# Running an expert's third matrix unit by unit beside the next expert's first two, with eight slots in the weight ring

## The chip, the cores and the metric

One core of a Trainium2 chip runs the whole kernel. The metric is device time in microseconds, the median of a few executions. Durations below come from one profiled execution.

## The reference

A two-layer block, then two layers of a second kind, for 256 tokens of width 1024 in fp32. The change touches only the mixture of experts in the second layer of the first block:

```python
def swiglu(x, w1, w3, w2):
    return (jax.nn.silu(x @ w1) * (x @ w3)) @ w2

def moe_ffn(x, router_w, w1, w3, w2):      # x: 256 x 1024, 8 experts, top 2
    logits = (xt @ router_w).astype(F32)
    top_v, top_i = lax.top_k(logits, TOP_K)
    top_w = jax.nn.softmax(top_v, axis=-1)
    gates = jnp.sum(jax.nn.one_hot(top_i, N_EXPERTS, dtype=F32) * top_w[..., None], axis=1)
    for e in range(N_EXPERTS):             # w1, w3: 1024 x 3584, w2: 3584 x 1024
        y = y + gates[:, e:e + 1] * swiglu(xt, w1[e], w3[e], w2[e])
```

## The kernel before

**Precision.** A weight block is used as a high and a low part. ScalarE copies the raw fp32 block into the high part (fp32r), VectorE subtracts it from the raw block and writes the low part over the raw one. Tokens are split likewise. A product then takes three matmuls: token high x weight high, token high x weight low, token low x weight high (`products`, L920).

**Units.** Expert weights come in units of 1 MB (128 x 2048 fp32), issued by SyncE in the order of use. An expert has 42: 28 for its first two matrices (w1, w3) and 14 for the third (w2). The raw ring has nine slots (`EXPERTS`, a `Ring`): seven of its own, the buffer `bias2` and the buffer `gain`. `gain` is away in rounds 2 and the start of 3, since round 2 keeps its hidden rows there, and again from unit 273 of 336 on (`GAIN_LENT`). The high parts have four slots, and both ScalarE (`ahead`, L1904) and VectorE (`split`, L2516) go at most three units ahead of TensorE (`EXPERT_LEAD`). A slot is free when TensorE has used its unit.

**Rounds.** Experts are sorted by how many tokens chose them. Even rounds r = 0, 2, 4, 6 take the larger ones, with up to 128 gathered tokens: 4 weight blocks a unit, 3 matmuls of 512 columns each, 12 in all. Odd rounds (`few`) take the smaller ones, with up to 64 tokens. There the token high parts fill 64 rows of the array's output and the low parts the other 64 (`gathered_few`), so 2 matmuls a block, 8 a unit, give all products. Round 2 (`LARGE`) does both for the largest expert: 20 a unit. Further rounds stand behind a branch and don't run with these inputs.

**A round, on TensorE.** `pair_e` (or `pair_few`, and for round 2 `many_tokens_e`) goes through w1 and w3 in tiles of 512 hidden columns, two tiles at a time in PSUM banks `tile0` to `tile3`. A finished tile goes through ScalarE (silu) and VectorE (product), and two units later TensorE transposes it (`turn`, L1045) into one of four `aux` banks, from where ScalarE and VectorE write it as hidden parts. In odd rounds ScalarE copies both raw tiles out and TensorE folds the two halves while it transposes (`fold_hidden`, L1389). When all seven tiles are through, the 14 units of w2 run, with their sums in `tile2` and `tile3`. ScalarE scales the output with the gate (`back_out`), VectorE adds the low part in odd rounds (`back_low`).

**Between rounds.** The output of round r - 1 is scattered back to token order behind unit 2 of round r (`scatter`, L1368, four banks), VectorE adds it to `acc` (L3068). The gates are turned behind unit 4 (`turn_gates`, L1351 and L1354), and in the rounds that gather, unit 4 of w2 is followed by the gather of the next one or two rounds' tokens (`gather`, L1340, eight banks in one go). Round 1 gathers for rounds 2 and 3, round 3 for 4 and 5, round 5 for 6 and 7.

Each engine has its own instruction stream and runs it in order; the order is written out by hand, and the streams meet in semaphores (`unit_done`, `high_ready`, `low_ready`, `aux_full`, `aux_evac`, `ye_ready`). The main loop of an odd round on TensorE shows the manner:

```python
for pair in range(PAIRS):
    def meanwhile(k):
        if k == TURN_AFTER and pair == 0:
            scatter_last(r)
        if k == TURN_AFTER and pair > 0:
            fold_hidden(2 * pair - 2)
            fold_hidden(2 * pair - 1)
        if k == PAIR_UNITS - 1 and pair == 0:
            turn_gates(r)
    pair_few(tiles[0:2], both, meanwhile)
    pair_few(tiles[2:4], both)
```

## Time and profile before

| | us |
|---|---|
| median of three executions | 2352.26 (2351.29 to 2354.27) |
| the profiled execution | 2352.72 |
| its span, first to last instruction | 2350.9 |
| the eight expert rounds | 442.0 to 1439.3 of the span |

The core's mean granted TensorE clock is 0.993. The page gives busy times over the whole span; the expert rounds are 42% of it, and the rest of the kernel is not touched. Round boundaries are the times at which TensorE's matmuls change from one expert's tokens to the next's. A matmul's own length in the timeline contains its pipeline; what it costs the stream is the distance of the starts. A row with a count merges instructions that follow each other.

### The profile page before, as it was taken

The page shows a single profiled execution, that of the slowest core. Times are in us where ns is not written, and L with a number is a line of the kernel's source. Part 1 is how long each engine was busy: PE and PEld are TensorE (multiplying, and loading weights), DVE is VectorE, ACT ScalarE, POOL GpSimd, SP SyncE. Part 2 cuts the span into 40 slices and gives each one's busy share as a digit, 9 for nine tenths or more (in the row PEclk, how much of TensorE's full clock was granted, in tenths as well). Part 3 has the DMA queues.
Part 4 walks back from the last instruction along what each step waited for, and adds up shares of the span by engine and source line. Part 5 has one row for each costly group of instructions (what it writes and reads, how often), then busy time and mean ns, then how long its engine had stood idle before and what let it go on. Part 6 is the DMA issues. An engine that isn't in the chain of part 4 may idle for free.

```text
span 2350.9 us, 29295 instructions
## 1 busy us (share of the span) xinstructions
PE 2304.0 (98%) x11179; PEld 1895.3 (81%) x11179; DVE 1810.5 (77%) x2343; ACT 1386.7 (59%) x1588; POOL 31.7 (1%) x44
## 2 busy tenths in 40 slices
PE   9999998999999999999999998999999999999998
PEld 7788887887878887788778776888888888888887
DVE  4965568798975558998999898899865669987655
ACT  4444544577865548877887785565544545654543
POOL 0000000000000000000000000000000000000000
PEclk9999999899999999999999999999999999999999
DMA  8366554699986569999999995654566565455653
GB/s 275 114 214 185 184 163 160 249 360 356 411 290 211 200 229 360 415 399 373 395 414 386 378 408 223 199 154 145 175 199 188 180 212 159 123 174 171 199 186 124
DMA packets 198508, 584.20 MB, mean 248 GB/s; under 512 B 17259, under 2 KB 26615, under 8 KB 183640
## 3 DMA queue, kind: packets, MB, share of 16 engines
q1 hardware_dynamic: 196060, 573.97, 68.8%
q0 software_dynamic: 1872, 6.82, 0.9%
q8 instruction: 91, 1.49, 0.3%
q10 hardware_dynamic: 428, 1.45, 0.2%
q14 instruction: 57, 0.47, 0.1%
HBM read 580.07 MB, written 2.12 MB: 248 GB/s over the span
## 4 chain that ended last, share of the span: by engine, by line
PE 81%; DVE 11%; ACT 6%; issue 2%; DMA 0%; POOL 0%; ACTq 0%; POOLq 0%; DVEq 0%
PE tile L922 21%; PE tile L924 21%; PE tile L923 21%; DVE units_parts L2527 5%; PE aux L1045 4%; PE aux L1389 3%; ACT high L1914 2%; PE tile L1503 2%; PE tile L1504 2%; ACT gbuf_parts L1914 1%; ACT acts L1914 1%; PE tile L1401 1%; PE aux L1786 1%; PE aux L1368 1%; DVE nat_parts L2527 1%
## 5 line engine op out<-in xcount | busy, mean ns | idle before, releaser
L2527 DVE TENSOR_TENSOR units_parts<-units,high 128x1024 fp32r<-128x1024 f32 (+3 forms) x339 | 482.6, 1442 | 94.9 <-ACT high L1914 92.0
L923 PE MATMUL tile<-units_parts,acts 128*128 128x512 f32 (+2 forms) x1352 | 518.5, 383 | 0.0
L1914 ACT ACTIVATE high<-units 128x1024 fp32r<-128x1024 f32 (+3 forms) x339 | 412.5, 1238 | 162.3 <-PE tile L924 57.0
L922 PE MATMUL tile<-high,acts 128*128 128x512 f32 (+2 forms) x1012 | 401.4, 397 | 6.3 <-DVE units_parts L2527 3.6
L924 PE MATMUL tile<-high,acts 128*128 128x512 f32 (+2 forms) x1012 | 390.3, 386 | 0.0
L923 PEld LDWEIGHTS tile<-units_parts,acts 128*128 128x128 f32 x1352 | 255.5, 189 | 46.7 <-issue 1.0
L922 PEld LDWEIGHTS tile<-high,acts 128*128 128x128 f32 x1012 | 191.2, 189 | 44.7 <-DVE units_parts L2527 6.2
L924 PEld LDWEIGHTS tile<-high,acts 128*128 128x128 f32 x1012 | 191.1, 189 | 38.8
L923 PE MATMUL tile<-units_parts,zbuf_parts 128*128 128x512 f32 x432 | 168.1, 389 | 0.0
L924 PE MATMUL tile<-high,zbuf_parts 128*128 128x512 f32 x368 | 143.3, 389 | 0.0
L922 PE MATMUL tile<-high,zbuf_parts 128*128 128x512 f32 x296 | 116.1, 392 | 0.0
L2527 DVE TENSOR_TENSOR units_parts<-units,acts 128x2048 fp32r<-128x2048 f32 x39 | 89.2, 2287 | 14.4 <-ACT acts L1914 14.3
L3279 DVE SCALAR_TENSOR_TENSOR zbuf<-cbuf,taps,zbuf 128x256 f32<-128x256 f32 x240 | 99.7, 479 | 0.0
L1945 ACT ACTIVATE acts<-aux 128x512 fp32r<-128x512 f32 x48 | 27.5, 597 | 120.8 <-PE aux L1045 120.7
L2527 DVE TENSOR_TENSOR units_parts<-units,gbuf_parts 128x2048 fp32r<-128x2048 f32 x39 | 89.2, 2287 | 11.6 <-ACT gbuf_parts L1914 11.6
L923 PEld LDWEIGHTS tile<-units_parts,zbuf_parts 128*128 128x128 f32 x432 | 81.2, 188 | 16.4
L1914 ACT ACTIVATE gbuf_parts<-units 128x2048 fp32r<-128x2048 f32 x39 | 74.7, 1916 | 29.6 <-PE tile L1403 13.0
L1914 ACT ACTIVATE acts<-units 128x2048 fp32r<-128x2048 f32 x39 | 74.8, 1918 | 12.6 <-PE tile L924 12.4
L1401 PE MATMUL tile<-high,params_parts 128*128 128x512 f32 x192 | 77.5, 404 | 3.9 <-DVE units_parts L2527 2.3
L924 PEld LDWEIGHTS tile<-high,zbuf_parts 128*128 128x128 f32 x368 | 69.1, 188 | 14.4
L2527 DVE TENSOR_TENSOR q_buf_parts<-q_buf,high 128x2048 fp32r<-128x2048 f32 x26 | 59.5, 2289 | 20.8 <-ACT high L1914 20.7
L1938 ACT ACTIVATE gbuf<-tile,row_scale 128x512 f32<-128x512 f32 x36 | 24.3, 687 | 80.7 <-PE tile L924 80.7
(565 smaller groups left out, 5078.1 us busy)
## 6 DMA issues: line engine op xcount, KB each, us to landing
units<-in_moe_w SPq DMA_DIRECT2D x156, 1024.0 KB, 8.0
units<-in_w_in SPq DMA_DIRECT2D x134, 512.0 KB, 3.9
units<-in_w_ff SPq DMA_DIRECT2D x128, 512.0 KB, 3.7
q_buf<-in_moe_w SPq DMA_DIRECT2D x39, 1024.0 KB, 7.8
k_buf<-in_moe_w SPq DMA_DIRECT2D x39, 1024.0 KB, 8.2
nat<-in_moe_w SPq DMA_DIRECT2D x39, 1024.0 KB, 8.1
bias<-in_moe_w SPq DMA_DIRECT2D x38, 1024.0 KB, 8.0
gain<-in_moe_w SPq DMA_DIRECT2D x25, 1024.0 KB, 8.4
```

The costliest lines, as they stand in the source:

```text
L922: nc.tensor.matmul(bank, lhs[0], high, start=start, stop=False)
L923: nc.tensor.matmul(bank, lhs[0], low, start=False, stop=False)
L924: return nc.tensor.matmul(bank, lhs[1], high, start=False, stop=stop)
L1045: mm = nc.tensor.transpose(bank[0:m, i * k:(i + 1) * k], src, ident[0:k, 0:k])
L1389: mm = nc.tensor.matmul(bank[:, at:at + FEW], raw[:, m, c * P:(c + 1) * P], fold[:, :], start=True, stop=True)
L1401: nc.tensor.matmul(bank[:, :], both[:, at_k, :], high[:, c, at], start=at_k == 0, stop=False)
L1503: nc.tensor.matmul(bank[:, :], both, high, start=at_k == 0, stop=False)
L1504: return nc.tensor.matmul(bank[:, :], both, low, start=False, stop=at_k == chunks - 1)
L1914: nc.scalar.activation(high_slot(SG[0], n) if wide_ else high_slot(SG[0], n)[:, 0:cols], halves(weights) if wide_ else weights[:, 0:cols], ...
L1945: nc.scalar.activation(dst, aux[k % 4][0:p, 0:n * m].rearrange("p (n m) -> p n m", n=n), ACT.Copy).then_inc(SG[0].turned_high, 1)
L2527: V.tensor_tensor(low, weights, high, ALU.subtract).then_inc(SG[0].low_ready, 1)
L3279: ins = V.scalar_tensor_tensor(y_t[:, c, :], u_t[:, c, j:j + SEQ], taps[:, c, j:j + 1], y_t[:, c, :], ALU.mult, ALU.add)
```

## The change

The rounds become steps (`step_units`). Step s runs the 28 units of the first two matrices of round s; behind each second one comes one of the 14 units of the third matrix of round s - 1. Step 0 has only first matrices, step 8 only the third matrix of round 7. The order of the loads, splits and matmuls is the same list for all engines.

The third matrix accumulates in `aux0` and `aux1`, and for the 64 further rows of round 2 in `tile2` and `tile3`; the first matrices of round 3 therefore use `tile0` and `tile1` alone. The other two `aux` banks (`spare`) serve in turn for all turns, folds, gates, scatters and gathers, with semaphores of their own (`spare_full`, `spare_evac`). A tile's turn comes behind units 9, 17 and 25 (two tiles each; in round 2 behind each fourth from 5 on), the last tile's behind unit 1 of the next step. The output of round r is scattered in step r + 2, behind units 3 and 5. A gather takes one bank behind each of the units 18 to 24 and 26 of the first matrices, for round 7's further rounds behind units 4 to 11 of its third matrix. Step 0 now has the gather for round 1, and VectorE's `find_order` behind its unit 11.

Buffers: `bias2` is no ring slot any more; it holds a third set of gathered tokens, the odd rounds' products, a selection table and scratch. The ring has eight slots with `gain`, seven without. `gain` is away in steps 2 and 3 and up to about unit 10 to 17 of step 4, and again from unit 273 on. The rules for leads (three units) and for the four high slots are the same.

```diff
--- before.py
+++ after.py
-EXPERT_COLS, EXPERT_UNITS, EXPERT_HIGHS = 2048, 9, 4
+EXPERT_COLS, EXPERT_UNITS, EXPERT_HIGHS = 2048, 8, 4
...
-GAIN_LENT = [(0, LARGE * MOE_UNITS, 1),
-             ((LARGE + 1) * MOE_UNITS + TURN_AFTER + 2 + EXPERT_OWN, (N_EXP - 2) * MOE_UNITS + MOE_UNITS // 2,
-              (LARGE + 1) * MOE_UNITS + TURN_AFTER + 2)]
-EXPERTS = Ring(ROUNDS * MOE_UNITS, (EXPERT_OWN + 1) * [[(0, ROUNDS * MOE_UNITS, 0)]] + [GAIN_LENT])
-GAIN_FREE = 1 + EXPERTS.last[EXPERT_OWN + 1]
+PAIRED, FIRST_UNITS = 2 * PAIRS * PAIR_UNITS, 2 * MOE_TILES * TILE_UNITS
+assert FIRST_UNITS == 2 * BACK_UNITS
+LAST_TILE = MOE_TILES - 1
+TAIL_AT, SCATTER_AT, GATES_AT = 1, (3, 5), 6
+CHOOSE_AT, GATHER_AT = 13, (18, 19, 20, 21, 22, 23, 24, 26)
+BACK_SCATTER, BACK_CHOOSE, BACK_GATHER = (2, 3), 2, (4, 5, 6, 7, 8, 9, 10, 11)
+STEP_UNITS = [FIRST_UNITS] + (N_EXP - 1) * [MOE_UNITS] + [BACK_UNITS]
+STEP_FIRST = [sum(STEP_UNITS[:i]) for i in range(N_EXP + 2)]
+GAIN_OPEN = STEP_FIRST[LARGE + 2] + SCATTER_AT[1] + SCATTER_AT[1] // 2 + 3
+GAIN_LENT = [(0, STEP_FIRST[LARGE], 1),
+             (GAIN_OPEN + EXPERT_OWN, (N_EXP - 2) * MOE_UNITS + MOE_UNITS // 2, GAIN_OPEN)]
+EXPERTS = Ring(ROUNDS * MOE_UNITS, EXPERT_OWN * [[(0, ROUNDS * MOE_UNITS, 0)]] + [GAIN_LENT])
+GAIN_FREE = 1 + EXPERTS.last[EXPERT_OWN]
...
+def step_units(s):
+    if s > N_EXP:
+        return [(s - 1, m) for m in range(MOE_UNITS)]
+    units = []
+    for i in range(FIRST_UNITS):
+        if s < N_EXP:
+            units.append((s, i))
+        if s > 0 and i % 2:
+            units.append((s - 1, FIRST_UNITS + i // 2))
+    return units
...
+def first_place(r, i):
+    if r == LARGE:
+        m, k = divmod(i % (2 * TILE_UNITS), TILE_UNITS)
+        return [i // (2 * TILE_UNITS)], m, k, [m]
+    if i < PAIRED:
+        pair, at = divmod(i, 2 * PAIR_UNITS)
+        m, k = divmod(at, PAIR_UNITS)
+        banks = [0, 1] if r == LARGE + 1 else [2 * m, 2 * m + 1]
+        return [2 * pair, 2 * pair + 1], m, k, banks
+    m, k = divmod(i - PAIRED, TILE_UNITS)
+    return [LAST_TILE], m, k, [m if r == LARGE + 1 else 2 * m]
+def closes(r, i):
+    return first_place(r, i)[2] == (PAIR_UNITS if r != LARGE and i < PAIRED else TILE_UNITS) - 1
...
+def turned_after(r, i):
+    if r == LARGE:
+        return [i // 4 - 1] if i >= 5 and i % 4 == 1 else []
+    return [i // 4 - 2, i // 4 - 1] if i >= 9 and i % 8 == 1 else []
...
-        gathered_few = [params_parts[:, i * 1024:(i + 1) * 1024].rearrange("p (c n) -> p c n", n=P)
-                        for i in range(2)]
+        bias2_flat, bias2_flat_parts = (v[:, :, :].rearrange("p h t -> p (h t)") for v in (bias2, bias2_parts))
+        gathered_few = [v.rearrange("p (c n) -> p c n", n=P) for v in
+                        (params_parts[:, 0:1024], params_parts[:, 1024:2048], bias2_flat_parts[:, 0:1024])]
...
+        spare = aux[2:4]
...
+            def expert(s, named):
+                for r, m in step_units(s)[EXPERT_FIRST if s == 0 else 0:]:
+                    expert_part(r, 0 if r == 0 else named[r - 1], m)
+                if s == 0:
                     sp.wait_ge(order_ready, 1)
                     at = 2 * EXTRA
                     named.extend(sp.value_load(extra[0:1, at + k:at + k + 1], min_val=0, max_val=N_EXP - 1)
                                  for k in [column_of(q) - 1 for q in range(1, N_EXP)])
-                if r < N_EXP - 1:
-                    units(r + 1, named[r], 0, EXPERT_LEAD)
-                if r >= N_EXP:
-                    multiplied(r)
+                if s > N_EXP:
+                    multiplied(s - 1)
...
+                    def spare_bank(*name):
+                        n = spare_at[name] = C.spare.take()
+                        wait(pe, spare_evac[n % 2], n // 2)
+                        return spare[n % 2]
...
+                    def take_bank(n, taken_out, value):
+                        if n in held:
+                            pe.wait_ge(*held[n])
+                        held[n] = taken_out, value
...
+                    def first_matrices(r, back, late):
+                        arrived = C.aux.n - 4
+                        for i in range(FIRST_UNITS):
+                            if r == 0 and i < 4:
+                                evacuated_to(arrived + i + 1)
+                            if i == 0:
+                                for q in range(r):
+                                    if r in gathered_by(q):
+                                        spare_done("gathered", q, 6)
+                                        spare_done("gathered", q, 7)
+                            first_unit(r, i)
+                            if back is not None and i % 2:
+                                back_unit(back, i // 2)
+                            if i == TAIL_AT and back is not None:
+                                turn_tile(back, LAST_TILE)
+                            if i in SCATTER_AT and late is not None:
+                                scatter(late, SCATTER_AT.index(i))
+                            if i == GATES_AT:
+                                turn_gates(r)
+                            for t in turned_after(r, i):
+                                turn_tile(r, t)
+                            if i in GATHER_AT and gathers_within(r):
+                                gather(r, GATHER_AT.index(i))
+                    def second_matrix(r, late):
                         for k in range(BACK_UNITS):
...
+                            back_unit(r, k)
+                            if k == TAIL_AT:
+                                turn_tile(r, LAST_TILE)
+                            if k in BACK_SCATTER and late is not None:
+                                scatter(late, BACK_SCATTER.index(k))
+                            if k in BACK_GATHER and gathers(r):
+                                gather(r, BACK_GATHER.index(k))
+                    def expert(s, _):
+                        if s < N_EXP:
+                            first_matrices(s, s - 1 if s > 0 else None, s - 2 if s > 1 else None)
+                        elif s == N_EXP:
+                            second_matrix(N_EXP - 1, N_EXP - 2)
+                        else:
+                            first_matrices(s - 1, None, s - 2)
+                            second_matrix(s - 1, None)
...
+            def passed(units):
+                C.unit.take(units)
+                split(min(C.unit.n + EXPERT_LEAD, limit[0]))
...
+            def add_spare(r, b):
+                for h in range(2):
+                    y = acc[:, b, h * 512:(h + 1) * 512]
+                    bank, evacuated_ = spare_in("scattered", r, b, h)
+                    V.tensor_tensor(y, y, bank[:, :], ALU.add).then_inc(evacuated_, 1)
...
+            def first_matrices(r, back, late):
+                folds = few(r) or r == LARGE
+                for i in range(FIRST_UNITS):
+                    passed(1)
+                    tiles_, m, _, banks = first_place(r, i)
+                    if r == LARGE:
+                        for t in lows_after(r, i):
+                            low_few(r, t)
+                    if closes(r, i) and m == 1 and not few(r):
+                        dve.wait_ge(S.unit_done, C.unit.n)
+                        for t, bank in zip(tiles_, banks):
+                            gate_hidden(r, t, bank)
+                    if back is not None and i % 2:
+                        passed(1)
+                    if i == TAIL_AT and back is not None:
+                        tile_in(back, LAST_TILE)
+                    if i == TAIL_AT + 2 and back is not None and (few(back) or back == LARGE):
+                        low_few(back, LAST_TILE)
+                    if i in SCATTER_AT and late is not None:
+                        add_spare(late, SCATTER_AT.index(i))
+                    for t in turned_after(r, i):
+                        tile_in(r, t)
+                    if few(r):
+                        for t in lows_after(r, i):
+                            low_few(r, t)
+                    if r == 0 and i == 3:
+                        V.tensor_scalar(acc[:, :, :], x[:, :, :], ALPHA, None, ALU.mult)
+                    if r == 0 and i in (7, 15):
+                        split_x((i - 7) // 8)
+                    if r == 0 and i == 11:
+                        find_order()
+                    if r == 4 and i == 15:
+                        find_extra()
+                    if i == CHOOSE_AT + (4 if r == 0 else 0) and gathers_within(r):
                         choose(gathered_lots(r), rank)
```

## Rows read from the trace of the kernel before

**Rows 1.** the page's first lines: the span, and busy time of an engine, share of the span, instructions
```profile
span 2350.9 us, 29295 instructions
...
PE 2304.0 (98%) x11179; PEld 1895.3 (81%) x11179; DVE 1810.5 (77%) x2343; ACT 1386.7 (59%) x1588; POOL 31.7 (1%) x44
```

**Rows 2.** windows, rounds 0 to 7: stretch, length, busy by engine, clock, DMA share, GB/s
```profile
442.00:563.50 121.50, 120.52 (x564) 99.90 (x563) 108.27 (x76) 89.74 (x68) 0.00 (x0) 1.00 0.92 352
563.50:668.60 105.10, 101.89 (x495) 80.03 (x493) 98.73 (x66) 94.09 (x98) 0.00 (x0) 1.00 1.02 405
668.60:881.70 213.10, 211.59 (x1000) 176.77 (x1001) 118.70 (x79) 102.40 (x93) 0.00 (x0) 0.99 0.64 216
881.70:989.10 107.40, 104.58 (x504) 81.42 (x502) 97.08 (x63) 92.03 (x89) 0.00 (x0) 1.00 0.97 386
989.10:1110.40 121.30, 120.94 (x547) 99.34 (x547) 112.81 (x93) 89.37 (x62) 0.00 (x0) 1.00 1.00 388
1110.40:1214.30 103.90, 101.14 (x495) 79.87 (x494) 98.56 (x64) 92.88 (x91) 0.00 (x0) 1.00 1.02 401
1214.30:1334.80 120.50, 120.48 (x547) 99.58 (x548) 109.44 (x64) 88.61 (x61) 1.64 (x3) 1.00 0.99 385
1334.80:1439.30 104.50, 101.43 (x495) 79.78 (x493) 95.92 (x61) 86.50 (x81) 0.00 (x0) 1.00 0.92 366
```

**Rows 3.** timeline of TensorE: start, length, line, out<-in, count [idle before]
```profile
479.75 0.39 PE L922 MATMUL tile<-high,acts 128*128 128x512 f32 x1
...
480.43 0.39 PE L922 MATMUL tile<-high,acts 128*128 128x512 f32 x1
...
681.48 0.44 PE L1351 MATMUL aux<-consts_sb,sc_parts 128*128 128x128 f32 x2 [1.37 <-DVE acc L3068]
...
702.62 0.60 PE L1045 MATMUL aux<-consts_sb,gbuf 128*128 128x128 f32 x4
703.06 1.90 PE L1389 MATMUL aux<-fold,gbuf 128*128 128x64 f32 x16
704.76 0.48 PE L922 MATMUL tile<-high,acts 128*128 128x512 f32 x1
...
994.72 2.12 PE L1368 MATMUL aux<-gbuf_parts,zbuf_parts 128*128 128x512 f32 x8
```

**Rows 4.** chain of work, by start: start, length, engine, tile, line, count
```profile
532.76 3.52 PE aux L1340 x32
...
587.02 3.53 PE aux L1389 x32
...
885.50 6.87 PE aux L1368 x16
```

**Rows 5.** timeline of VectorE in round 5
```profile
1136.14 2.28 DVE L2527 TENSOR_TENSOR units_parts<-units,high 128x2048 fp32r<-128x2048 f32 x1
1138.35 0.75 DVE L3089 TENSOR_TENSOR zbuf<-zbuf,aux 128x256 f32<-128x256 f32 x2
1139.76 2.29 DVE L2527 TENSOR_TENSOR units_parts<-units,acts 128x2048 fp32r<-128x2048 f32 x1 [0.67 <-ACT acts L1914]
```

**Rows 6.** transfers in 900:980, then in 700:860: issues, size, median us to landing
```profile
DMA packets 7761, 32.93 MB, mean 412 GB/s; under 512 B 504, under 2 KB 504, under 8 KB 5963
...
nat<-in_moe_w SPq DMA_DIRECT2D x4, 1024.0 KB, 11.4
...
k_buf<-in_moe_w SPq DMA_DIRECT2D x4, 1024.0 KB, 5.0
```

**Rows 7.** windows, the first two matrices of round 0
```profile
442.00:523.50 81.50, 80.92 (x371) 66.47 (x369) 76.64 (x59) 61.63 (x45) 0.00 (x0) 1.00 0.97 369
```

**Rows 8.** timeline of ScalarE in round 5
```profile
1122.19 1.10 ACT L2121 ACTIVATE zbuf<-tile 128x512 f32<-128x512 f32 x2
1123.15 1.95 ACT L1914 ACTIVATE high<-gain 128x2048 fp32r<-128x2048 f32 x1
```

More of the change, by code:

```diff
@@ L869, in _ @@
                     sp.wait_ge(S.aux_full, SCORED1)
-                    units(0, 0, 0, EXPERT_FIRST, len(STREAM1))
+                    for m in range(EXPERT_FIRST):
+                        expert_part(0, 0, m, len(STREAM1) + m)
                     wide(S, A["w_out"][l], D - P, P)
@@ new lines, in _, with products_few @@
+                    held, gated_before = {}, C.gated.n
+                    def take_bank(n, taken_out, value):
+                        if n in held:
+                            pe.wait_ge(*held[n])
+                        held[n] = taken_out, value
+                    def products_few(bank, both, high, low, start, stop):
+                        nc.tensor.matmul(bank[:, :], both, high, start=start, stop=False)
+                        return nc.tensor.matmul(bank[:, :], both, low, start=False, stop=stop)
@@ L1654, in _ @@
             pe.wait_ge(last_ye, 1)
-            scatter(N_EXP - 1)
+            for b in range(TB):
+                for h in range(2):
+                    scatter_bank(aux_bank(), N_EXP - 1, b, h).then_inc(S2.aux_full, 1)
             keep_busy(9)
@@ new lines, in second_matrix @@
+            def second_matrix(r, late):
+                for k in range(BACK_UNITS):
+                    passed(1)
+                    if k == TAIL_AT:
+                        tile_in(r, LAST_TILE)
+                    if k == TAIL_AT + 2:
+                        low_few(r, LAST_TILE)
+                    if k in BACK_SCATTER and late is not None:
+                        add_spare(late, BACK_SCATTER.index(k))
+                    if k == BACK_CHOOSE and gathers(r):
+                        choose(gathered_lots(r), rank)
+                back_low()
```

902 lines of the change are left out of this document (322 added, 580 removed).

## Prediction

> **What bounds the kernel now.** I read the page's busy times first, then the busy time by expert round, then durations inside rounds. The page says TensorE is busy 98% of the span and VectorE 77% [rows 1]; that average hides where anything can be won, since a matmul that starts late still counts as busy. The change touches only the eight expert rounds, 442 to 1439.3 us. By round they take 121.5, 105.1, 213.1, 107.4, 121.3, 103.9, 120.5 and 104.5, together 997.3 us [rows 2]. The even ones but round 2 hold up to 128 tokens (three matmuls a weight block, 12 a unit), the odd ones up to 64 (8 a unit), round 2 both kinds (20 a unit). Every round has 42 units.
>
> TensorE starts three 512-column matmuls in 0.68 us, 0.227 each [rows 3]. So a unit costs it 2.72, 1.82 or 4.54 us. An even round is 504 x 0.227 = 114.4 us of matmuls and with its small work as long as measured: TensorE bounds it. An odd round is only 42 x 1.82 = 76.4. To that come seven folds (two are 3.53), a gather (3.52) and a scatter of the even round's output (16 matmuls for round 2's two kinds 6.87, so 3.4 for the eight of the others) [rows 4] and gates (estimate 0.6, from the 0.44 of their transposes [rows 3]): 76.4 + 12.4 + 3.5 + 3.4 + 0.6 = 96.3, and 99.8 in round 3. The four take 420.9 against 388.7: TensorE lacks 32 us there. Rounds 0, 2, 4 and 6 lack some 4 more.
>
> What it lacks is VectorE's low half of a unit. VectorE subtracts one unit each 2.21 us, and between them has products, with 0.67 us of idling behind ScalarE [rows 5]; 42 x 2.21 = 92.8, and its busy time in odd rounds is 95.9 to 98.7 of some 105. The transfers are as full: share 1.02 and 405 GB/s in round 1; in round 2 they idle, 0.64 and 216 GB/s [rows 2]. A round's 42 units are 44.0 MB, at 412 GB/s [rows 6] 106.9 us. So odd rounds stand at two limits, VectorE's and the transfers', while even rounds and round 2 stand at TensorE's.
>
> **The change part by part.** No large matmul, split or load goes or comes. The order changes: step s runs the 28 units of the first two matrices of round s, and after each second one a unit of the third matrix of round s - 1. Step 0 has 28 units, steps 1 to 7 have 42, step 8 has 14. I price each step's work on TensorE.
>
> Small terms: fold 1.76 a tile, turn 0.44 (702.62 to 703.06), both together 2.14 (702.62 to 704.76), scatter of an odd round 2.0 [rows 3], of an even one 3.4, of round 2 6.9, gather 3.5 [rows 4].
> - Step 0: the same part took 81.5 [rows 7]; the gather moves into it: 85.0.
> - Step 1: 28 x 1.82 + 14 x 2.72 = 89.1; six folds 10.6, a turn 0.4, gather 3.5, gates 0.6: 104.2.
> - Step 2: 28 x 4.54 + 14 x 1.82 = 152.6; six turns with folds 12.8, a fold 1.8, scatter 3.4, gates 1.2: 171.8.
> - Step 3: 28 x 1.82 + 14 x 4.54 = 114.6; 10.6 + 2.1 + 2.0 + 3.5 + 0.6: 133.4.
> - Step 4: 28 x 2.72 + 14 x 1.82 = 101.7; turns 2.6, fold 1.8, scatter of round 2 6.9, gates 0.6: 113.6.
> - Step 5: 89.1 + 10.6 + 0.4 + 2.0 + 3.5 + 0.6 = 106.2.
> - Step 6: 101.7 + 2.6 + 1.8 + 3.4 + 0.6 = 110.1.
> - Step 7: as 5 without the gather, 102.7. Step 8: 25.5 + 1.8 + 3.4 + 3.5 = 34.2.
>
> The sum is 961.2, or 36.1 less than 997.3. That is all the lack there is, and needs the other engines to keep up.
>
> Do they? VectorE, per step: the mean of an even and an odd round's busy time, (112.8 + 98.6) / 2 = 105.7 with rounds 4 and 5 and 102.7 with 6 and 7 [rows 2], against 102.7 to 113.6. It no longer bounds a step, but is 93 to 100% full. Odd rounds show what such a full loop costs: 103.9 to 107.4 us for 96 to 99 us of VectorE's work, 6 to 9% on top; even rounds with 109.4 to 112.8 of 121 lose under 1%. I take a little over 1% of the 671 us of steps 1 and 4 to 8: +8 (bounds 0 and 6%, 40). The transfers need 106.9 a step: 2.7 more than TensorE in step 1, 0.7 in step 5, 4.2 in step 7, and in step 8 (14.7 MB, 35.6) 1.4, together 9.0; a ring full at the start of such a step lends two or three units, 5 to 7 us. I take +5 (bounds 0 and 9).
>
> The Trainium skill, DMA: Bandwidth & Descriptors, section Measured, gives 425 GB/s to a core that streams alone; by that figure, called an estimate, the transfers would need 103.6 us a step and the +5 would be near 0. The trace's 412 over 80 us is below it, and the sum goes by the trace.
>
> *Slots.* Ring slots go from nine to eight, seven while the gain buffer is away: steps 2 and 3, the first units of step 4, and from unit 273 to the end, 63 units. The trace shows 11.4 us to landing with nine slots and a full queue, 5.0 us where TensorE is slow [rows 6]; most of the 11.4 is queue. A slot is held 5.0 (landing) + 1.9 (ScalarE's copy [rows 8]) + 2.2 (VectorE) + 2.5 us (TensorE) without any lead and 7.5 more with three finished units waiting: 19.1 / 7 = 2.73 us a unit with the full lead, 1.7 with none. TensorE asks for 2.45 to 2.7 there. Round 3 started with eight slots and took 107.4, 3.4 of which is the longer scatter; so the ninth slot bought nothing measurable. I take 0 (bounds 0 and 63 x 0.28 = 18).
>
> *Banks.* Turns, folds, gates, scatters and gathers now share two spare PSUM banks in place of four, since the third matrix gets two of its own. Queued behind a bank wait on TensorE is the next unit. Most takes are a unit (1.8 to 4.5 us) apart, which covers the reader's 0.4 to 0.7 us. Not covered: step 2 turns its first tile right behind a scatter. The gates behind a scatter waited 1.37 us for VectorE [rows 3]; I take 1.4 (bounds 0 and 5).
>
> *Gathers and scatters.* The gather was one block of eight banks, behind which ScalarE fell late; it is now a bank a unit. Same work, perhaps 2 us gained an odd round, which is in the lack already counted. Scatters and VectorE's additions move a step later and two units on, hidden by the lead. SP's queue keeps one order, and only in step 0 it waits for the expert order (written in round 0 as now), with the first 28 units already issued or waiting for slots: nothing.
>
> *Round 3's banks.* In step 3 the first matrices have two tile banks, which ScalarE must empty before the next matrix; a unit of round 2's third matrix (4.54 us) lies between, longer than two copies and one high half on ScalarE (1.1 + 1.9 [rows 8]): nothing.
>
> Sum: 961.2 + 8 + 5 + 1.4 = 975.6, so 21.7 less. The profiled execution took 2352.7 us (span 2350.9 [rows 1] and 1.8 around it), 0.5 above the median of 2352.26. 2352.7 - 21.7 = **2331.0 us**.
>
> **The rivals.**
> *All idle time goes.* The allowances come out near nothing: 2316.6 to 2322. For it: even rounds run at 1% of TensorE's sum. Against: VectorE has slack of 5% here and 8 to 10% there.
> *The loops stay coupled.* VectorE, ScalarE and transfers are all over 90% full, and waits in order cost half of what they cost odd rounds, 3 to 4% of 671 us, 20 to 25: 2342 to 2347. For it: the 0.67 us behind ScalarE, in each odd round's eight units [rows 5].
> *Too few slots, slower than before.* Place: unit 273 onward, with seven slots. If landing stays long while the lead is held, a slot turns over in 11.4 + 1.9 + 2.2 + 7.5 + 2.5 = 25.5 us, 3.6 a unit with seven and 3.2 with eight. 63 x 1.1 + some 119 units (steps 1, 4 late, 5, 6 to 273) x 0.6 = 141 worst; half of it gives 961 + 70 + 8 = 1039: 2394. It decides from a loss of 36 us, that is a landing time of about 8 us under full lead. Against: 5.0 us in round 2, and TensorE's wait would eat up the lead first.
> *The memory gives less over a long stretch.* Rounds that pull 405 are short. If 450 us of steps 4 to 8 and step 1 ran at round 7's 366 GB/s [rows 2], a step takes 120.3: +16.1, 6.7, 14.1, 10.2, 17.6, 5.9 are 70.6 in all, 961.2 + 70.6 = 1031.8: 2387. Against: rounds 4 and 5 moved 388 and 401 over 225 us, with the ring and not the memory as their limit. The Trainium skill, DMA: Bandwidth & Descriptors, section Specifications, states a limit of about 358 GB/s for one core, by which the time would be still longer. The trace's 405 over round 1 disagrees.
>
> **How the numbers follow.** Forecast (2322 to 2340) 0.55; all idle gone 0.13; coupled (2340 to 2347.5) 0.14; within 0.2%, as a mix of these losses, 0.06; too few slots 0.10; memory 0.02. A measurement of this kernel can tell about 0.2% (4.7 us) from no change. Faster 0.82, same 0.06, slower 0.12. The range 2316 to 2350 leaves out the two slower cases and a bit.
>
> **What the profile after would show.** Step lengths as listed: step 2 near 173, step 3 near 134, steps 1 and 5 to 7 at 104 to 112. VectorE busy near 95% in each; the transfers' share over 0.95 from step 4 on and no longer 0.64 in the large round's stretch alone but some 0.7 to 0.8 over steps 2 and 3. TensorE's starts 0.227 apart with few gaps. Landing falls from 11 to 7 to 9 us. Wrong if: step 7 and 8 stretch past 115 and 40 (slots); TensorE waits for VectorE's additions or products more than 1 us at many takes (banks); or the matmuls of mixed units start further apart than 0.227.

## The result, and the profile of the changed kernel

| | kernel before | changed kernel |
|---|---|---|
| median, 15 executions each | 2351.80 us | 2356.87 us |
| lowest to highest | 2345.81 to 2354.27 | 2352.04 to 2363.86 |
| profiled execution, span | 2350.9 us | 2356.7 us |
| expert part, in its span | 439.9 to 1439.3: 999.4 us | 440.0 to 1443.9: 1003.9 us |

The ratio is 1.0027, with a 95% interval of 1.0017 to 1.0038. The kernel became 0.3% slower, where 0.9% faster was forecast (2331.0, range 2316 to 2350). The busy times tell nothing of it. The first lines of the page of the changed kernel, to be held against [rows 1]:

```profile
span 2356.7 us, 29360 instructions
...
PE 2299.1 (98%) x11179; PEld 1906.0 (81%) x11179; DVE 1811.6 (77%) x2343; ACT 1385.4 (59%) x1588; POOL 31.7 (1%) x44
...
units<-in_moe_w SPq DMA_DIRECT2D x180, 1024.0 KB, 7.2
```

The windows of the changed kernel, step 0 to step 8, stand against [rows 2]: stretch, length, busy time by engine, clock, DMA share, GB/s.

```profile
440.00:526.00 86.00, 83.63 (x402) 69.83 (x401) 77.23 (x62) 63.05 (x53) 0.00 (x0) 1.00 0.90 335
526.00:633.00 107.00, 106.36 (x531) 88.73 (x530) 98.96 (x60) 92.92 (x93) 0.00 (x0) 1.00 1.02 400
633.00:813.40 180.40, 176.19 (x830) 146.47 (x828) 112.54 (x77) 101.49 (x95) 0.00 (x0) 0.98 0.72 249
813.40:948.60 135.20, 135.20 (x666) 114.37 (x667) 105.62 (x66) 94.05 (x91) 0.00 (x0) 0.99 0.90 326
948.60:1066.00 117.40, 115.57 (x512) 93.21 (x511) 106.67 (x91) 87.53 (x62) 0.00 (x0) 0.99 0.96 369
1066.00:1179.10 113.10, 109.61 (x539) 91.20 (x538) 102.63 (x65) 92.78 (x88) 0.00 (x0) 0.98 1.01 399
1179.10:1292.00 112.90, 111.15 (x504) 90.25 (x503) 103.01 (x63) 86.93 (x64) 1.64 (x3) 1.00 1.00 385
1292.00:1408.70 116.70, 107.70 (x506) 86.86 (x506) 106.00 (x62) 94.06 (x77) 0.00 (x0) 0.99 1.00 393
1408.70:1443.90 35.20, 34.82 (x168) 27.68 (x168) 29.90 (x22) 23.61 (x22) 0.00 (x0) 1.00 0.68 253
```

The change did what it says: VectorE's and the transfers' work is now spread evenly, VectorE at 91 to 93% in steps 1 and 4 to 7. But against the work foretold for TensorE (85.0, 104.2, 171.8, 133.4, 113.6, 106.2, 110.1, 102.7, 34.2; sum 961.2) the nine steps are longer by 1.0, 2.8, 8.6, 1.8, 3.8, 6.9, 2.8, 14.0 and 1.0 us: 42.7, where 14.4 were allowed. In the prediction's terms the excess of 28.3 us, less 0.8 for the rest of the kernel (1352.8 for 2350.9 - 997.3 = 1353.6), is the error of 27.5 us against the profiled execution (2356.7 and 1.8 around it, for 2331.0).

Two figures of the prediction rest on a boundary that was read too late. The first expert matmul of the kernel before, and the one for which TensorE waits in step 0 of the changed kernel:

```profile
439.94 0.48 PE L922 MATMUL tile<-gbuf_parts,acts 128*128 128x512 f32 x1
```

```profile
496.80 0.66 PE L1398 MATMUL aux<-sc_parts,x_high 128*128 128x128 f32 x4 [2.37 <-DVE sc_parts L2992]
```

So the expert part before took 999.4 us and not 997.3, and the change costs 4.5 us there and 1.3 us in the rest. The first matrices of round 0 took 80.1 us (439.9 to 520.0) and not 81.5. Step 0's work is then 83.6, and what it lost is 2.4 us: the wait of the gather for its selection table, which VectorE writes behind its subtractions. The nine steps are 44.1 us over the work, not 42.7.

Where TensorE waited in steps 1 to 8, the eight largest of thirteen rows (engine, tile, line, what it waited for, then us in all, times, longest):

```profile
PE aux L1429 <- DVE acc L3027: 5.0, 2, 2.7
PE aux L984 <- DVE gbuf_parts L3054: 2.9, 2, 2.0
PE tile L1485 <- DVE gbuf L3061: 2.2, 1, 2.2
PE aux L1485 <- ACT gbuf L2192: 2.2, 1, 2.2
PE aux L1461 <- DVE acc L3027: 2.0, 1, 2.0
PE tile L984 <- DVE units_parts L2467: 1.8, 1, 1.8
PE aux L984 <- DVE units_parts L2467: 1.6, 4, 0.8
PE tile L984 <- DVE k_buf_parts L2467: 1.3, 1, 1.3
```

L1429 and L1461 are the gates' transposes and the turn: they want a spare bank that VectorE's addition of a scatter (L3027) has not read yet, in steps 5, 7 and 2. The two `aux` rows behind them, L984 on L3054 and L1485 on L2192, are the output banks `aux0` and `aux1` of the preceding third matrix, not emptied when the next third matrix wants them, at the starts of steps 5, 7 and 8. L1485 on L3061 is the tile bank that VectorE's last hidden product of round 2 has to read before step 3 can take it. Of the waits of 1.3 us and more, it and L1485 on L2192, which is ScalarE's read of an output bank, are the two that VectorE's stream doesn't explain. Before the wait at step 3 VectorE had been idle for 2.97 us, for a small operation of ScalarE (L2116) that stood behind ScalarE's copy of a unit (start, length, engine, line):

```profile
809.84 1.91 ACT L1883 ACTIVATE high<-k_buf 128x2048 fp32r<-128x2048 f32 x1
812.08 0.42 DVE L3048 TENSOR_TENSOR gain_parts<-bias,gain_parts 128x256 fp32r<-128x256 f32 x1 [2.97 <-ACT gain_parts L2116]
813.36 0.77 PE L1485 MATMUL tile<-gbuf_parts,params_parts 128*128 128x512 f32 x1 [2.24 <-DVE gbuf L3061]
```

The 1.8 is step 4, behind VectorE's `find_extra` (4.3 us of small operations).

The wait in step 5, on TensorE (start, length, line, tile, [idle before]):

```profile
1090.03 0.39 PE L1486 MATMUL tile<-units_parts,params_parts 128*128 128x512 f32 x1
1092.77 0.44 PE L1429 MATMUL aux<-consts_sb,sc_parts 128*128 128x128 f32 x2 [2.36 <-DVE acc L3027]
...
1094.30 0.63 PE L1486 MATMUL tile<-units_parts,params_parts 128*128 128x512 f32 x1
1094.73 0.63 PE L1485 MATMUL tile<-high,params_parts 128*128 128x512 f32 x1
```

On VectorE in the same stretch:

```profile
1084.24 1.27 DVE L3027 TENSOR_TENSOR acc<-acc,aux 128x512 f32<-128x512 f32 x2
1085.44 4.48 DVE L2467 TENSOR_TENSOR units_parts<-units,high 128x2048 fp32r<-128x2048 f32 x2
1089.84 2.28 DVE L2467 TENSOR_TENSOR units_parts<-units,acts 128x2048 fp32r<-128x2048 f32 x1
1092.04 1.27 DVE L3027 TENSOR_TENSOR acc<-acc,aux 128x512 f32<-128x512 f32 x2
```

And the windows of that stretch, with columns as above:

```profile
1092.00:1094.00 2.00, 1.23 (x7) 1.23 (x8) 2.00 (x4) 0.10 (x1) 0.00 (x0) 0.77 1.02 408
1094.00:1096.00 2.00, 2.00 (x5) 1.53 (x5) 1.52 (x1) 2.00 (x3) 0.00 (x0) 0.50 1.04 418
```

Two things are to be seen. The additions are short, 0.6 us each, but they stand in VectorE's stream behind three subtractions without a gap, 6.6 us; a bank handed over in unit 5 is returned when VectorE gets there, and TensorE, at the gates of unit 6, stands still. And when TensorE goes on, its clock is halved: the granted clock is 0.50 of full (1.2 of 2.4 GHz) and the starts are 0.43 us apart instead of 0.227. Five such stretches lie in the expert part, four of 3.4 us and one of 6.8, 20.4 us in all. Windows inside the other four, in steps 2, 3, 4 and 7:

```profile
673.30:680.00 6.70, 6.70 (x27) 6.12 (x26) 1.36 (x3) 3.18 (x4) 0.00 (x0) 0.50 0.23 87
813.20:816.50 3.30, 3.14 (x8) 2.50 (x9) 3.30 (x3) 1.80 (x2) 0.00 (x0) 0.50 0.96 343
1028.30:1031.60 3.30, 3.30 (x9) 2.51 (x9) 3.30 (x3) 0.00 (x0) 0.00 (x0) 0.50 1.02 407
1321.80:1325.10 3.30, 3.30 (x8) 2.55 (x9) 2.95 (x2) 2.25 (x3) 0.00 (x0) 0.50 0.95 379
```

Before there is one of 3.4 us, behind the one gates' wait of 1.37 us [rows 3]. At half clock a share of (0.427 - 0.227) / 0.427 = 0.47 is lost: 9.6 us.

### The profile page after: what moved, and what is told of

It is laid out like the page before. It is cut to its first block, busy times and chain, and to the rows that moved or that the text cites. A ratio compares the mean times of both kernels' runs of the same rounds, so it can differ in the third digit from the quotient of the medians.

```text
span 2356.7 us, 29360 instructions
## 1 busy us (share of the span) xinstructions
PE 2299.1 (98%) x11179; PEld 1906.0 (81%) x11179; DVE 1811.6 (77%) x2343; ACT 1385.4 (59%) x1588; POOL 31.7 (1%) x44
## 4 chain that ended last, share of the span: by engine, by line
PE 87%; DVE 8%; ACT 2%; DMA 2%; issue 1%; POOL 0%; POOLq 0%; SPq 0%; ACTq 0%; DVEq 0%
PE tile L984 19%; PE tile L986 19%; PE tile L985 19%; PE tile L1485 5%; PE tile L1486 5%; PE aux L1107 3%; DVE units_parts L2467 3%; PE aux L1471 3%; PE aux L1485 2%; PE aux L1486 2%; PE aux L984 2%; PE aux L986 2%; PE aux L985 2%; PE aux L1398 1%; PE aux L1755 1%
## 5 line engine op out<-in xcount | busy, mean ns | idle before, releaser
L2467 DVE TENSOR_TENSOR units_parts<-units,high 128x1024 fp32r<-128x1024 f32 (+3 forms) x351 | 509.8, 1470 | 94.4 <-ACT high L1883 91.8
L1883 ACT ACTIVATE high<-units 128x1024 fp32r<-128x1024 f32 (+3 forms) x351 | 435.8, 1260 | 148.6 <-DMA units<-in_w_in 40.6
L984 PE MATMUL tile<-high,acts 128*128 128x512 f32 (+2 forms) x1024 | 405.1, 396 | 9.5 <-DVE units_parts L2467 5.6
L984 PEld LDWEIGHTS tile<-high,acts 128*128 128x128 f32 x1024 | 193.1, 189 | 48.3 <-DVE units_parts L2467 7.9
L985 PE MATMUL tile<-units_parts,zbuf_parts 128*128 128x512 f32 x328 | 127.7, 389 | 0.0
L2467 DVE TENSOR_TENSOR units_parts<-units,acts 128x2048 fp32r<-128x2048 f32 x45 | 102.9, 2286 | 19.5 <-ACT acts L1883 19.3
L2467 DVE TENSOR_TENSOR units_parts<-units,gbuf_parts 128x2048 fp32r<-128x2048 f32 x45 | 102.9, 2287 | 8.0 <-ACT gbuf_parts L1883 7.6
L986 PE MATMUL tile<-high,zbuf_parts 128*128 128x512 f32 x256 | 99.7, 390 | 0.0
L1914 ACT ACTIVATE acts<-aux 128x512 fp32r<-128x512 f32 x48 | 27.5, 597 | 122.3 <-PE aux L1107 122.3
L1486 PE MATMUL tile<-units_parts,params_parts 128*128 128x512 f32 x244 | 97.7, 401 | 0.0
L1883 ACT ACTIVATE gbuf_parts<-units 128x2048 fp32r<-128x2048 f32 x45 | 86.6, 1924 | 17.6 <-PE tile L986 5.8
L2467 DVE TENSOR_TENSOR k_buf_parts<-k_buf,high 128x2048 fp32r<-128x2048 f32 x33 | 75.5, 2288 | 13.8 <-ACT high L1883 13.7
L1485 PE MATMUL tile<-high,params_parts 128*128 128x512 f32 x208 | 84.0, 404 | 0.7 <-DVE nat_parts L2467 0.5
L984 PE MATMUL tile<-high,zbuf_parts 128*128 128x512 f32 x184 | 72.2, 393 | 0.0
L985 PEld LDWEIGHTS tile<-units_parts,zbuf_parts 128*128 128x128 f32 x328 | 61.7, 188 | 12.4
```

The lines of the kernel that those rows point to most:

```text
L984: nc.tensor.matmul(bank, lhs[0], high, start=start, stop=False)
L985: nc.tensor.matmul(bank, lhs[0], low, start=False, stop=False)
L986: return nc.tensor.matmul(bank, lhs[1], high, start=False, stop=stop)
L1485: nc.tensor.matmul(bank[:, :], both, high, start=start, stop=False)
L1486: return nc.tensor.matmul(bank[:, :], both, low, start=False, stop=stop)
L1883: nc.scalar.activation(high_slot(SG[0], n) if wide_ else high_slot(SG[0], n)[:, 0:cols], halves(weights) if wide_ else weights[:, 0:cols], ...
```

## The experiments

Each ratio is to runs of the kernel before on the same chip, with its 95% interval. "Halved" experiments leave work out, as their expectations say.

**The slots.** The kernel before with the changed kernel's ring.

```diff
-EXPERT_COLS, EXPERT_UNITS, EXPERT_HIGHS = 2048, 9, 4
+EXPERT_COLS, EXPERT_UNITS, EXPERT_HIGHS = 2048, 8, 4
-EXPERTS = Ring(ROUNDS * MOE_UNITS, (EXPERT_OWN + 1) * [[(0, ROUNDS * MOE_UNITS, 0)]] + [GAIN_LENT])
+EXPERTS = Ring(ROUNDS * MOE_UNITS, EXPERT_OWN * [[(0, ROUNDS * MOE_UNITS, 0)]] + [GAIN_LENT])
```

> The order of before, with the ring of the change: eight slots, seven while the gain buffer is away (the bias2 slot is dropped). Theory H (hand-overs: TensorE loses its gain at waits for spare banks, output banks and the last gate, and by half-clock stretches behind them): the slots cost nothing here, 2350 to 2356 us. Theory S (fewer slots starve the loads): odd rounds, which run at the transfers' rate, get longer by 3 us or more each, 2362 us or more.

Measured: 1.0012 [0.9997, 1.0027]; rounds 1 to 6 take 105.3, 212.9, 108.6, 121.3, 103.9, 120.5. Of these only round 3, which begins with seven slots, is longer, by 1.2. Round 7, with seven slots throughout, is longer by 1.2 as well: 105.3 for 104.1, from its first matmul to its last. That is 2.4 us in the profiled execution, and the median can't tell it from nothing.

The changed kernel with seven slots nearly everywhere. `gain` was to be out of the ring, but took part for a single unit:

```diff
-GAIN_LENT = [(0, STEP_FIRST[LARGE], 1),
-             (GAIN_OPEN + EXPERT_OWN, (N_EXP - 2) * MOE_UNITS + MOE_UNITS // 2, GAIN_OPEN)]
+GAIN_LENT = [(9, 10, 9)]
```

> The changed kernel with the gain buffer never in the ring: seven slots throughout, so steps 0, 1 and 4 to 6 lose one too. Theory H: within 3 us of the changed kernel, 2354 to 2360. Theory S: if the seventh-slot stretch is why step 7 took 116.7 us against a sum of 102, steps 1, 5 and 6 lose like it, 6 to 8 us each, 2372 or more.

Measured: 1.0105 [1.0075, 1.0135]. But steps 0 and 1 took 100.4 and 111.8, and the waits of that stretch show an artefact of the edit: that one unit was loaded late, and everything stood behind it.

```profile
ACT high L1883 <- DMA gain<-in_moe_w: 14.2, 1, 14.2
...
PE tile L984 <- DVE gain_parts L2467: 9.5, 1, 9.5
```

So this run says nothing of the slots as a whole. The clean form has `GAIN_LENT = [(0, 0, 0)]`:

> Seven slots throughout, this time without the slip of the first attempt, in which a single unit (the tenth) still used the gain slot and was loaded so late that TensorE waited 9.5 us for it in step 0. The slip theory: the whole +15 us was that unit, so this one is within 3 us of the changed kernel, 2350 to 2358. Slot theory: 2365 or more again, with steps 1, 5 and 6 longer by 5 us each.

Measured: 1.0048 [1.0030, 1.0066], steps 1 to 7 at 109.4, 180.6, 135.3, 116.4, 113.8, 114.2, 115.3. Beside the changed kernel's 1.0027 that is some 5 us for a slot less in the steps that had eight (2.4 in step 1, 1.3 in step 6), and the intervals overlap. The changed kernel with its eighth slot kept to the end of step 7:

```diff
-             (GAIN_OPEN + EXPERT_OWN, (N_EXP - 2) * MOE_UNITS + MOE_UNITS // 2, GAIN_OPEN)]
+             (GAIN_OPEN + EXPERT_OWN, STEP_FIRST[N_EXP], GAIN_OPEN)]
```

> The changed kernel with the gain buffer in the ring up to the end of step 7's last unit (before: unit 273), so eight slots through step 7. Theory S: step 7 falls from 116.7 to 108 or less, 2349 or less, unless the later load of the gain row shows up behind the experts. Theory H: step 7 within 2 us of 116.7, total 2355 to 2360.

Measured: 1.0029 [1.0014, 1.0044], no change beside 1.0027, though steps 6 and 7 were 2.6 and 3.9 us shorter in the profiled execution (110.3 and 112.8). The mean granted clock of its ten executions was 0.9882 against the changed kernel's 0.9899; on that, see the last section. Two things stand against the gain. Step 8 was 2.2 us longer (37.4 for 35.2). And the two profiled executions are not the medians: the one of the changed kernel lay 1.6 above its median (2358.5 for 2356.87), this one 2.9 below its own (2354.54 for 2357.41). The slots don't explain the loss.

**The hand-overs.** Gates two units later, and in step 2 the scatter behind units 2 and 3, so that the turn no longer follows it at once.

```diff
-TAIL_AT, SCATTER_AT, GATES_AT = 1, (3, 5), 6
+TAIL_AT, SCATTER_AT, GATES_AT = 1, (3, 5), 8
+def scatter_at(r):
+    return (2, 3) if r == LARGE else SCATTER_AT
```

> The changed kernel with uses of the spare banks moved apart: gates turned behind unit 8 in place of 6, in the large step the two scatters behind units 2 and 3 in place of 3 and 5. Theory H: the three waits for VectorE's additions (1.98, 2.36 and 2.66 us) and the half-clock stretches behind them (about 1.7 us each) go: 10 to 12 us less than the changed kernel, 2345 to 2348. Rival V (VectorE is short of time, a wait removed comes back at the next unit): less than 4 us gained, 2353 or more.

Measured: 0.9975 [0.9960, 0.9991], 12 us less than the changed kernel by the ratios (0.0052 of 2352, give or take some 4 us by their intervals). The same view of TensorE's waits, steps 1 to 8:

```profile
PE aux L989 <- DVE gbuf_parts L3059: 3.4, 2, 2.1
PE tile L1490 <- DVE gbuf L3066: 2.2, 1, 2.2
PE aux L1490 <- ACT gbuf L2197: 2.2, 1, 2.2
PE tile L989 <- DVE units_parts L2472: 2.1, 2, 1.8
```

The rows with `acc`, 5.0 and 2.0 us, are gone, and the half-clock stretches fall from 20.4 to 10.2 us, worth 4.8. Together that is 11.8. The match is in part luck. The removed waits took 13.6 us of half clock with them. Of what is left, the stretch in step 4 is missing in this execution though its wait of 1.84 us is there, and two of 3.4 us follow waits of 2.06 and 2.21 us, at the start and the end of step 7, that had none in the changed kernel. Same work, same engines, same slots: two constants took the kernel from slower than before to faster.

**The transfers.** Each expert load brings half of its columns. ScalarE copies that half twice into the high part, and VectorE subtracts the high part from itself over the full width, so their operations keep number and size (the diff shows the load alone).

```diff
+                d = dst(memory)
+                if expert_unit(sig_, n) >= 0:
+                    c = d.shape[1] // 2
+                    d, src = d[:, 0:c, :], src[:, 0:c, :]
-                sp.dma_start(dst(memory), src).then_inc(loaded, 16)
+                sp.dma_start(d, src).then_inc(loaded, 16)
```

> The changed kernel with each expert load halved: it moves the first 1024 of 2048 columns, ScalarE reads that half twice, and VectorE subtracts the high half from itself instead of reading the raw block; the count and size of all engine instructions are as before (the expert outputs are not the reference's). Theory T (what is left to lose, 25 us beside the hand-overs, is the transfers' rate of 107 us a step): steps 1, 5 and 7 fall to 104, 107 and 106, 12 to 20 us less, 2337 to 2345. Theory V (VectorE's order: a small operation stands behind up to three splits of 2.2 us): under 5 us less, 2352 or more.

> The kernel before with the same halved loads. If its odd rounds stand at the transfers' rate, they fall from 104 to 107 to about 98 us, 2325 to 2335 in all. If they stand at VectorE's, nothing moves: 2347 to 2353.

Measured: changed kernel 1.0003 [0.9986, 1.0020], kernel before 1.0001 [0.9985, 1.0018]. The first window is step 5 of the changed kernel with half the bytes, the second round 5 of the kernel before with half the bytes:

```profile
1062.00:1175.60 113.60, 109.61 (x539) 91.10 (x538) 103.20 (x65) 92.84 (x88) 0.00 (x0) 0.98 0.65 196
```

```profile
1109.20:1213.10 103.90, 101.15 (x495) 79.88 (x494) 98.56 (x64) 92.89 (x91) 0.00 (x0) 1.00 0.67 210
```

The DMA share falls from 1.01 and 1.02 to 0.65 and 0.67. Round 5 takes 103.9 us with 401 GB/s and with 210; step 5 takes 113.1 and 113.6. For the kernel before, the transfers bound nothing. For the changed kernel this is not settled. The 0.24% between the ratios, 5.6 us, is at the edge of what the intervals can tell. In the profiled execution steps 6 and 7 are 1.8 and 3.5 us shorter (111.1 and 113.2), steps 0 and 8 are 1.6 and 1.5 longer (87.6 and 36.7), and the others differ by 1.0 at most. In step 7, with seven slots, ScalarE waited some 12 us in all for loads in the changed kernel, and not once with half the bytes. So late loads may have cost up to 3.5 us in that step.

**VectorE.** It subtracts one half of each unit, and TensorE reads that half twice (the diff shows VectorE's part).

```diff
-                        weights, low = halves(weights), halves(low)
+                        weights, low, high = (v[:, 0, :] for v in (halves(weights), halves(low), high))
```

> The changed kernel with VectorE's split of each expert unit halved (it writes the low part of 1024 of 2048 columns, TensorE reads that half twice; expert outputs are not the reference's). Loads are whole. Theory V: the waits for additions, output banks and products go with their half-clock stretches, some 20 to 30 us less, 2327 to 2337, and steps 1, 5 and 7 end at the transfers' 104 to 108. Theory T: 5 to 10 us less, since the transfers stay: 2347 or more.

> The kernel before with the same halved splits. If VectorE alone bounds its odd rounds, they fall from 105 to 97 to 99 us each (TensorE's sum is 96 to 100), 2322 to 2330. If the transfers bound them as well, they stop at 103 to 106: 2345 or more.

Measured: kernel before 0.9910 [0.9890, 0.9931], changed kernel 0.9938 [0.9917, 0.9958]. Round 5 of the kernel before with halved subtractions:

```profile
1098.20:1196.50 98.30, 97.31 (x495) 81.11 (x494) 57.60 (x63) 89.71 (x89) 0.00 (x0) 1.00 1.02 403
```

VectorE's busy time falls from 98.6 to 57.6 us and the round from 103.9 to 98.3, with the DMA share still at 1.02. Rounds 1 and 3 went from 105.1 and 107.4 to 99.1 and 104.1. So VectorE was what odd rounds lacked; but freeing it brings 21 us on the whole, not 36. Evening out VectorE's load leaves all of its work in place, so it could hardly have brought more than that. In this run TensorE's largest wait in the expert part is for ScalarE's copies in front of the folds, 3.8 us in six waits. In the changed kernel the halved work brings 21 us as well, and the hand-over waits stay in part (gates behind additions 3.7 us in two, the turn 0.9, output banks 2.5 and 1.7). The wait at step 3 stays whole, 2.2 us: VectorE's load was not its cause.

Both edits together, spaced hand-overs and halved subtractions:

> The changed kernel with the spare banks' uses moved apart and VectorE's splits halved as well (expert outputs are not the reference's). If hand-overs and VectorE's share are two separate losses, both gains add up: 2357 less 13 less 21, 2320 to 2326. If the spacing only helped because VectorE was short of time, the sum is no better than the halved splits alone: 2331 to 2336.

Measured: 0.9918 [0.9899, 0.9938], beside 0.9938 and 0.9975 for the one and the other alone. The two gains overlap: with VectorE free the additions come sooner anyway. Steps 0 to 7 took 943.3 us against 927.0 of work foretold.

**A version that beats both.** First the spaced kernel with the eighth slot kept to the end of step 7:

> The changed kernel with the spare banks' uses moved apart and the gain buffer in the ring up to the end of step 7. With the slots at no cost it stays at the 2344 of the spaced kernel, within 2 us. If the seventh slot costs what the profile of the late kernel showed in steps 6 and 7 (6.5 us), 2337 to 2340.

Measured: 0.9976 [0.9966, 0.9987], no gain over 0.9975. Its trace shows where the slot's gain went. Step 6 takes 110.3 for 113.0, but at the end of step 7 TensorE waits 5.3 us for round 6's output, where the spaced kernel waits 2.2. ScalarE's read of that output (L2197) stands behind its copies of the next units, and one of these waited for its load:

```profile
1388.76 1.91 ACT L1888 ACTIVATE acts<-nat 128x2048 fp32r<-128x2048 f32 x1 [1.06 <-DMA nat<-in_moe_w]
1395.02 0.77 PE L1490 MATMUL aux<-high,zbuf_parts 128*128 128x512 f32 x1 [5.33 <-ACT gbuf L2197]
```

Then the same, with round 7's third matrix summed in `tile0` and `tile1`, which are free in step 8, so that it need not wait for round 6's output:

```diff
+        def out_bank(r, h):
+            return tiles[h] if r == N_EXP - 1 else aux[h]
-                                take_bank(4 + h, ye_ready, out_first + h + 1)
+                                take_bank((0 if r == N_EXP - 1 else 4) + h, ye_ready, out_first + h + 1)
```

> As the one before, and round 7's third matrix sums in tile banks 0 and 1, which are free by then, in place of the two output banks: the wait of 2.2 us at the start of step 8, where the banks still hold round 6's output, and the half-clock stretch behind it (1.7 us) go. Hand-over theory: 3 to 4 us below the one before. If the wait moves on to another, within 1 us of it.

Measured: 0.9963 [0.9952, 0.9973], median 2341.21 where the kernel before had 2347.87 on that chip. The window is its step 7, the rows are three of its four largest in steps 1 to 8 (the fourth, 2.1 in two, is late low halves):

```profile
1280.50:1387.40 106.90, 104.89 (x508) 86.02 (x506) 100.03 (x60) 87.33 (x70) 1.64 (x3) 1.00 1.02 411
```

```profile
PE tile L1494 <- DVE gbuf L3070: 2.2, 1, 2.2
PE tile L993 <- DVE units_parts L2476: 2.2, 2, 1.8
PE aux L993 <- DVE gbuf_parts L3063: 2.1, 2, 1.3
```

Of the waits for output banks of 2 us and more none is left, one half-clock stretch of 3.4 us remains in the expert part, and step 7 takes 106.9 for 116.7 in the changed kernel. A part of this moves on: step 8 takes 39.1 where the spaced kernel has 36.8 and the changed one 35.2, with new waits of 1.6 us for a low half and 1.8 us for VectorE's product of a folded tile. The gain over the spaced kernel is 0.12%, and 2.2 us over the version before this one on the same chip, both with overlapping intervals; that it beats the changed kernel (1.0027) and the kernel before is clear.

## Why the prediction was wrong

| step | work foretold | changed | spaced | best version | spaced, halved subtractions |
|---|---|---|---|---|---|
| 0 | 85.0 | 86.0 | 85.3 | 85.3 | 83.4 |
| 1 | 104.2 | 107.0 | 106.9 | 106.9 | 105.4 |
| 2 | 171.8 | 180.4 | 175.0 | 175.0 | 175.0 |
| 3 | 133.4 | 135.2 | 135.3 | 135.4 | 135.3 |
| 4 | 113.6 | 117.4 | 116.4 | 116.4 | 113.7 |
| 5 | 106.2 | 113.1 | 110.4 | 110.4 | 107.6 |
| 6 | 110.1 | 112.9 | 113.0 | 110.4 | 110.6 |
| 7 | 102.7 | 116.7 | 113.1 | 106.9 | 112.3 |
| 8 | 34.2 | 35.2 | 36.8 | 39.1 | 34.5 |

Step 0's 85.0 is 1.4 too high, as the section on the result shows. Step 8 runs to the last matmul of round 7's third matrix.

*What bounds the kernel: half right.* "Odd rounds stand at two limits, VectorE's and the transfers'": VectorE's yes, by the halved subtractions. The transfers' no, in the kernel before: a share of 1.02 was read as a limit, and half the bytes left round 5 at 103.9 us. For the changed kernel the +5 is neither confirmed nor refuted: half the bytes brought 5.6 us by the ratios, at the edge of the intervals, and nothing in step 5.

*The work foretold and the lack: too much was hoped for.* With VectorE freed, round 5 takes 98.3 us in the old order where 96.3 was added up, round 3 104.1 for 99.8. The "lack of 36 us" was inferred by subtraction and ascribed to VectorE whole; freeing VectorE gives back 21. The rest is spacing that the small terms of the sum don't hold: in the new order with VectorE freed, steps 0 to 7 still take 16 us more than foretold. Some 15 us of the 36 were not VectorE's to give.

*"It no longer bounds a step", +8: near for late low halves, far too low for what a full VectorE costs.* VectorE's load was foretold rightly (102.6 to 106.7 us a step from 4 to 7; 102.7 to 105.7 foretold), but at 91 to 93% with a lead of three units each small operation in its stream comes late by the subtractions ahead of it. In the list of waits, low halves of units come late by 6.1 us in all, 1.8 of it behind `find_extra`, and the selection table in step 0 by 2.4. But halving VectorE's subtractions takes 21 us out of the changed kernel, where 8 and 1.4 were allowed: the waits for banks and the clock hang on the same full stream.

*"Banks", +1.4 (0 to 5): the step that failed most.* It argued that takes a unit apart are covered, since the reader needs 0.4 to 0.7 us, and priced only step 2. It counted the reader's length, not what stands ahead of it. Waits for the additions took 7.3 us in steps 2, 5 and 7 and, for 0.3 of it, 8. The output banks, of which the prediction has no term at all, took 5.1: two units now lie between one third matrix and the next, and none before step 8, where before it was 28. That keeping two constants further apart brought 12 us shows this step; the output banks' share is argued from the rows and from the last version alone.

*"Round 3's banks", nothing: wrong at the step's start.* It argued that a unit of 4.54 us lies between a bank's last matmul and its next. At the first unit of step 3 it is round 1's last unit, 1.8 us, and the readers are ScalarE and then VectorE, with a copy of 1.91 us in front: 2.2 us, in every version.

*The clock: missing.* The text held [rows 3] with a 1.37 us wait and priced it at 1.37. The 3.4 us at half clock behind it cost 1.6 more in the kernel before, and such stretches cost 9.6 us in the changed one.

These are 6.1 + 2.4 + 7.3 + 5.1 + 2.2 + 9.6 = 32.7 of the 44.1 us. The other 11.4 are small spacings that no row names, and their cause stays open. In the kernel with spaced hand-overs and VectorE freed, rows name 10.3 us of waits and 1.6 us of half clock of the 17.7 us by which steps 0 to 7 are over (16.3 and step 0's 1.4); 5.8 are left. So about half of them were gone there.

*Slots, 0 (bounds 0 and 18): right* within what the runs tell: 2.4 us in the profile of the old order and nothing by its median, some 5 us for seven slots throughout in the new one. The landing time was foretold as 7 to 9 us and is 7.2. What was wrong is the rival: no run shows a shortage of slots that costs more than some 5 us, where it needed 36. *The memory rival* is out too: 399 and 393 GB/s in steps 5 and 7, and half the bytes leave step 5 at 113.6. The limit of about 358 GB/s for one core that the Trainium skill states (DMA: Bandwidth & Descriptors, section Specifications) is passed by these two steps for over 100 us each.

*The rival "the loops stay coupled"* had the mechanism, waits in order between full engines, but priced it at 20 to 25 us for steps 1 and 4 to 8. These have 31 us of excess, the clock's part included, and steps 0, 2 and 3, which it left out, 11. What came true was none of the rivals: it was the lack of 36 us read too high, the banks and the coupling too cheap, and two things without a term, the output banks and the clock.

Step 7 stays near 113 us wherever round 7's third matrix takes `aux0` and `aux1`. With the eighth slot that is the wait for them at its end, which grows from 2.2 to 4.7 and 5.3 us; without it the step would be at 108 and 107. With VectorE freed the wait is 2.8 us, and ScalarE waits some 16 us for loads in this step, with seven slots; that the loads hold it there is likely, but was not shown. Open are the 11.4 us above, and ScalarE as a limit of its own: it is busy for 75 to 87% of steps 1 and 4 to 7, and no run halves its work.

## What to carry to other kernels

A hand-over costs the reader's place in its stream, not its length: list what stands ahead of each short operation that returns a bank, on every engine that reads it, and keep as many units between the two takes of a bank as the reader's engine may be behind; here two constants were worth 12 us. Before a gain is booked as "what the engine lacks", halve the suspected engine's work and look, since a difference between a span and a sum of counted work holds the errors of the sum too. A busy share near 1 is no bound until halving the work moves the time.

## What the runs showed of the hardware

*A wait of TensorE costs more than its length.* Of the seven waits of 1.8 us and more in the expert part of the changed kernel five (1.98, 2.24, 1.83, 2.36, 2.66 us) were followed, within two microseconds, by 3.4 or 6.8 us at half clock, with starts 0.43 us apart; the two of 2.05 and 2.21 us at the start and the end of step 7 were not. A stretch of 3.4 us costs 1.6 us. The same wait isn't followed each time. Step 4's of 1.8 us was in the changed kernel, but not in the spaced one, in the best version and with half the bytes. The gates' 1.37 us was in the kernel before, but not the same wait of 1.36 us with half the bytes.

*The chain behind the wait in step 2* (start, length, what):

```profile
670.07 2.29 DVE units_parts L2467
672.36 0.61 DVE acc L3027
672.97 0.14 issue
673.10 0.97 PE aux L1461 x4
674.07 3.31 PE aux L1471 x16
677.38 0.53 PE tile L984
```

A 0.61 us addition behind a 2.29 us subtraction; then the fold, 3.31 us for 16 matmuls at half clock where two folds, 32 matmuls, took 3.53 before [rows 4], and large matmuls 0.43 apart.

*The mean clock goes with the spread of the executions.* The 15 executions of the changed kernel run from 2352.04 us at a mean granted clock of 0.993 over 2356.87 at 0.990 to 2363.86 at 0.987: 2.1 us for each thousandth, with a correlation of -0.97. A mean lower by a thousandth is 4.7 us at half clock, of which 0.47 is 2.2. The means over the executions are 0.9899 for the changed kernel, 0.9932 spaced, 0.9932 for the best version, and 0.9935 to 0.9947 for the kernel before on four chips. Between the first and the last lie 3.6 to 4.8 thousandths, some 8 to 10 us; the stretches in the expert part of the two traces, 20.4 and 3.4 us, give 8.0.

*The DMA share as a measure.* It stood at 1.02 with 401 GB/s and at 0.67 with 210: half the bytes still show two thirds of the share, and neither bounded that round.
